# Gate matrix of a PEER layer: third block kept in SBUF, the others stored in 4 KB runs and fetched by four tiles, with new places for loads and dots

## What is computed

```python
def _peer(x, w_query, sub_keys, w_down, w_up):       # x: 512 tokens x 1024
    q = (x @ w_query).reshape(n_tok, 8, 2, 128)
    sc = einsum('thpk,hpnk->thpn', q, sub_keys)        # 8 heads, 2 sides, 128 keys
    va, ia = top_k(sc[:, :, 0], 16); vb, ib = top_k(sc[:, :, 1], 16)
    cand = va[..., :, None] + vb[..., None, :]
    top, flat = top_k(cand, 16)
    expert = ia[flat // 16] * 128 + ib[flat % 16]      # 128 experts per token, of 16384
    gate = softmax(top)
    act = gelu(einsum('tkd,td->tk', w_down[expert], x))
    return einsum('tk,tkd->td', gate * act, w_up[expert])
x = layernorm(alpha * x + peer(x))
```

## Time and profile before

| | |
|---|---|
| median of 3 executions | 1749.91 us (1749.54 to 1751.03) |
| profiled execution, time / span | 1752.79 / 1751.0 us |
| busy, share of span: TensorE, VectorE, ScalarE, GpSimd | 92%, 70%, 36%, 46% |
| moved by DMA | 428 MB, mean 244 GB/s |
| mean granted TensorE clock | 0.963 of full |
| down stage in `peer_block` / up stage (matmuls) | 526 to 1188 / 1206 to 1731 us |

### The profile page before, as it was taken

How to read it: one execution, slowest core, us unless ns; L and a number is a source line. 1 busy time by engine, 2 the same in 40 slices (tenths; PEclk the granted TensorE clock), 3 DMA queues, 4 the chain that set the end, 5 groups by cost and what they waited for, 6 DMA issues and landing times.

```text
span 1751.0 us, 22553 instructions
## 1 busy us (share of the span) xinstructions
PE 1610.9 (92%) x8252; PEld 1435.8 (82%) x8252; DVE 1233.3 (70%) x2110; ACT 623.1 (36%) x807; POOL 799.1 (46%) x468
## 2 busy tenths in 40 slices
PE   7999978869979999998999899685999999999995
PEld 6787857758869999998999899674888888888884
DVE  2643442256989889788978895346888888888887
ACT  4223324222224355443544454132333333333331
POOL 7443642123318866686568566675222222222220
PEclk9999989889999999999999999897999999999997
DMA  8422322114226776797679667999999999999993
GB/s 296 156 96 85 117 76 96 34 50 146 83 66 188 260 245 200 245 364 263 205 257 362 248 201 272 372 347 386 376 352 355 357 355 351 355 354 354 355 351 147
DMA packets 195414, 428.08 MB, mean 244 GB/s; under 512 B 17009, under 2 KB 116593, under 8 KB 194801
## 3 DMA queue, kind: packets, MB, share of 16 engines
q1 hardware_dynamic: 106944, 262.78, 43.2%
q0 software_dynamic: 36864, 134.23, 21.0%
q10 hardware_dynamic: 51504, 29.71, 5.6%
HBM read 372.13 MB, written 54.53 MB: 244 GB/s over the span
## 4 chain that ended last, share of the span: by engine, by line
PE 53%; DMA 3%; ACTq 2%; POOL 2%; issue 1%; DVE 1%; ACT 0%; DVEq 0%
PE ps L1178 10%; PE ps L1179 10%; PE ps L1180 10%; PE ps L892 6%; PE ps L894 6%; PE ps L893 6%; PE ps L1150 3%; PE ps L1152 2%; ACTq L1086 2%; DMA gate_d<-gmat 2%; DMA rows<-in_w_down,expert 1%; POOL w_lo L1029 1%; POOL rows L1037 1%; DVE gmat L1353 0%; DVE gmat L1350 0%
## 5 line engine op out<-in xcount | busy, mean ns | idle before, releaser
L1029 POOL TENSOR_TENSOR w_lo<-raw,w_hi 128x1024 fp32r<-128x1024 f32 x127 | 324.9, 2564 | 186.4 <-ACT w_hi L1061 185.8
L892 PE MATMUL ps<-b_hi,w_hi 128*128 128x384 f32 x1024 | 354.4, 346 | 33.6 <-POOL w_lo L1029 33.6
L1061 ACT ACTIVATE w_hi<-raw 128x1024 fp32r<-128x1024 f32 x252 | 266.5, 1057 | 319.8 <-PE ps L1180 315.9
L893 PE MATMUL ps<-b_lo,w_hi 128*128 128x384 f32 x1024 | 347.7, 340 | 0.0
L894 PE MATMUL ps<-b_hi,w_lo 128*128 128x384 f32 x1024 | 347.6, 339 | 0.0
L1178 PE MATMUL ps<-w_hi,b_hi 128*128 128x512 f32 x768 | 299.9, 390 | 18.5 <-DVE b_lo L1268 18.5
L1037 POOL DMA_INDIRECT rows<-in_w_up,expert x128 | 128.9, 1007 | 386.8 <-DVE ps L1275 378.9
L1179 PE MATMUL ps<-w_lo,b_hi 128*128 128x512 f32 x768 | 299.5, 390 | 0.0
L1180 PE MATMUL ps<-w_hi,b_lo 128*128 128x512 f32 x768 | 299.5, 390 | 0.0
L182 POOL TENSOR_TENSOR w_lo<-raw,w_hi 128x1024 fp32r<-128x1024 f32 x60 | 152.9, 2556 | 199.2 <-ACT w_hi L210 199.2
L1197 DVE SCALAR_TENSOR_TENSOR rows<-rows,ps 128x1024 f32<-128x1024 f32 x128 | 155.0, 1219 | 107.5 <-DMA rows<-in_w_down,expert 100.9
(11 more groups left out here) (205 smaller groups left out, 2572.1 us busy)
## 6 DMA issues: line engine op xcount, KB each, us to landing
raw<-in_down_t SPq DMA_DIRECT2D x128, 512.0 KB, 3.8
raw<-in_up_t SPq DMA_DIRECT2D x128, 512.0 KB, 5.4
raw<-in_units SPq DMA_DIRECT2D x76, 512.0 KB, 3.2
act_d<-act_t SPq DMA_DIRECT2D x128, 192.0 KB, 4.4
gate_d<-gmat ACTq DMA_DIRECT2D x48, 512.0 KB, 10.1
gmat<-act_d SPq DMA_DIRECT2D x128, 192.0 KB, 4.6
gmat<-gate_d SPq DMA_DIRECT2D x128, 192.0 KB, 5.8
xt_raw<-in_x_t SPq DMA_DIRECT2D x1, 2048.0 KB, 12.3
```

Source lines behind the costliest of these rows:

```text
L892: nc.tensor.matmul(out, ring.w_hi[:, s, w], b_hi[:, c, 0:DT], start=c == 0, stop=False)
L893: nc.tensor.matmul(out, ring.w_hi[:, s, w], b_lo[:, c, 0:DT], start=False, stop=False)
L1029: nc.gpsimd.tensor_tensor(w_lo[:, s, :], raw[:, s, :], w_hi[:, s, :].bitcast(F32), ALU.subtract).then_inc(split_done, 1)
L1061: nc.scalar.activation(w_hi[:, u % W4, :], raw[:, u % W4, :], ACT.Copy).then_inc(hi_done, 1)
```

## The change

In words. (1) Only blocks 0 and 1 (`KEPT = 2`) of the gate matrix are stored, as runs of 4 KB in each partition, two pieces a tile in the first eight tiles of the following block; block 2 stays in `gmat`. (2) The stored gates are fetched for four tiles by one 512 KB DMA into the arrays `v16` and `i16` by turns, the activations by a DMA a tile into five slots `h_t` in `c0`. (3) The product is made in place, in two instructions, one for blocks 0 and 1, one for block 2. (4) The first loads of the up stage are issued at down tile 104 and not 123. Activations and gates then have new places in SP's loop. (5) Each block has 14 dots before its gate rounds instead of 8; `low(0)` and `low(1)` stand before the last seven dots. (6) The start value of `acc` comes from `xb` in PSUM and not from a load of `x_d`; the copy of `xb` stands behind tile 3 and not ahead of tile 0. (7) `xres` and the norm's weights use the part of `gmat` whose tiles are done, and are loaded at up tile 112.

```diff
-        steps += [t0 + 4, t0 + 6, t0 + 8, t0 + 10] + [t0 + 12, t0 + 13, t0 + 14, t0 + 15]
+        steps += [t0 + i for i in (4, 4, 5, 5, 7, 7, 8, 8, 13, 13, 14, 14, 15, 15)]
...
-            def load_gated(j):
-                if j >= W4:
-                    sp.wait_ge(h_ready, j - W4 + 1)
+            def load_act(j):
+                if j >= HS:
+                    sp.wait_ge(h_split, j - HS + 1)
                 sp.wait_ge(act_stored[j % ACTS], 16 * (j // ACTS) + 16)
-                sp.dma_start(act_u[:, j % W4, :], t["act_d"][j]).then_inc(ag_full[j % W4], 16)
-                sp.dma_start(gate_u[:, j % W4, :], t["gate_d"][j]).then_inc(ag_full[j % W4], 16)
+                sp.dma_start(h_t[:, j % HS, :], t["act_d"][j]).then_inc(act_full[j % HS], 16)
+
+            def load_gates(g):
+                if g >= 2:
+                    sp.wait_ge(h_ready, 2 * GG * (g - 1))
+                sp.dma_start(gate_u[g % 2], t["gate_d"][:, :, g * GG * P:(g + 1) * GG * P].rearrange(
+                    "b a (u j) -> a b u j", u=GG)).then_inc(gate_full[g % 2], 16)
...
-                if u == TILES - 5:
-                    sp.wait_ge(gate_stored, 16 * PIECES * DB)
-                    for j in range(W4):
-                        load_gated(j)
-                    sp.dma_start(xres[:, GB, :], t["x2_d"][GB]).then_inc(xg_full, 16)
-            for j in range(W4, 2 * W4):
-                load_gated(j)
-            for j in range(TILES - 2 * W4):
-                load(TILES + j + 2 * W4)
-                load_gated(j + 2 * W4)
+                if u == TILES - 24:
+                    sp.wait_ge(picks_ready, DB)
+                    sp.wait_ge(gate_stored, 16 * PIECES * KEPT)
+                    load_gates(0)
+                    load_gates(1)
+                    for j in range(HS):
+                        load_act(j)
+            for j in range(TILES):
+                if j + 2 * W4 < TILES:
+                    load(TILES + j + 2 * W4)
+                if j + HS < TILES:
+                    load_act(j + HS)
+                if j % GG == GG - 1 and j // GG + 2 < TILES // GG:
+                    load_gates(j // GG + 2)
+                if j == TILES - 16:
+                    sp.wait_ge(h_ready, 2 * late_tiles)
...
-                if u >= LEAD + BLOCK_TILES and b < DB and i < PIECES:
-                    store_piece(b - 1, i)
-                if b == DB and i < PIECES // 2:
-                    store_piece(DB - 1, 2 * i)
-                    store_piece(DB - 1, 2 * i + 1)
-                if u == TILES - 2:
+                if u >= LEAD + BLOCK_TILES and b < DB and i < PIECES // 2:
+                    store_piece(b - 1, 2 * i)
+                    store_piece(b - 1, 2 * i + 1)
+                if u == TILES - 8:
                     h_high(0)
                     h_high(1)
...
-                top_experts(nc, step, done, k, b, lambda: dots_until(made[0] + 1))
+                top_experts(nc, step, done, k, b, lambda: dots_until(made[0] + 2))
...
-                dots_until(first + 8)
+                dots_until(first + 14)
...
             def product(j):
...
+                of = h_t[:, s, :].rearrange("p (b j) -> p b j", b=DB)
+                nc.vector.scalar_tensor_tensor(out=of[:, 0:KEPT, :], in0=of[:, 0:KEPT, :], scalar=1.0 / GSCALE,
+                                               in1=gate_u[g % 2][:, :, j % GG, :], op0=ALU.mult, op1=ALU.mult
+                                               ).then_inc(h_ready, 1)
+                nc.vector.scalar_tensor_tensor(out=of[:, KEPT, :], in0=of[:, KEPT, :], scalar=1.0 / GSCALE,
+                                               in1=gmat[:, j, :], op0=ALU.mult, op1=ALU.mult).then_inc(h_ready, 1)
```

More of the change, by code:

```diff
@@ L882 @@
 PIECES = 16
+HS = 5
+GG = 4
+KEPT = DB - 1
 PB = NK // PIECES
@@ L951, in peer_block @@
         acc = ps[:, XB:XB + 2, :]
+        h_t = c0[:].rearrange("p h c -> p (h c)")[:, 0:HS * DT].rearrange("p (s j) -> p s j", s=HS)
+        gate_u = [x[:].rearrange("p b s i -> p (b s i)").rearrange("p (b u j) -> p b u j", b=KEPT, u=GG)
+                  for x in (t["v16"], t["i16"])]
         flat_g = gmat[:].rearrange("p b j -> p (b j)")
[L954 to L957, removed]
+        xres = flat_g[:, 0:TB * D].rearrange("p (b d) -> p b d", b=TB)
+        lng, lnb = flat_g[:, TB * D:TB * D + D], flat_g[:, TB * D + D:TB * D + 2 * D]
+        late_tiles = (TB + 2) * D // P
         def h_slot(of, s):
@@ L973, in peer_block @@
         gate_stored = sem("gate_stored")
-        ag_full = [sem(f"ag_full{i}") for i in range(W4)]
+        act_full = [sem(f"act_full{i}") for i in range(HS)]
+        gate_full = [sem(f"gate_full{i}") for i in range(2)]
         h_ready, h_hi_done, h_split = sem("h_ready"), sem("h_hi_done"), sem("h_split")
-        coef_done, xg_full, x2_full, ln_full = sem("coef_done"), sem("xg_full"), sem("x2_full"), sem("ln3_full")
+        coef_done, x2_full, ln_full = sem("coef_done"), sem("x2_full"), sem("ln3_full")
+        xb_full = sem("xb_full")
         block_done, res_added = sem("block4_done"), sem("res4_added")
@@ L1085, in store_piece @@
                     act.wait_ge(half_free, halves * (b + 1))
[L1086 to L1087 removed]
+                act.dma_start(t["gate_d"][b, :, PB * i * P:(PB * i + PB) * P],
+                              gmat[:, PB * i:PB * i + PB, :].rearrange("p b j -> p (b j)")).then_inc(gate_stored, 16)
             def h_high(j):
[L1090 removed]
+                act.wait_ge(h_ready, 2 * j + 2)
                 if j >= 2:
                     act.wait_ge(tile_done, TILES + max(0, j - W4 + 1))
[L1093 removed]
+                nc.scalar.activation(h_slot(b_hi, j % W4), h_t[:, j % HS, :].rearrange("p (b j) -> p b j", b=DB),
                                      ACT.Copy).then_inc(h_hi_done, 1)
[L1096 to L1097 removed]
             for u in range(TILES):
@@ L1101, in _ @@
                 b, i = divmod(u - LEAD, BLOCK_TILES)
+                if u == W4 - 1:
+                    act.wait_ge(xb_full, 16)
+                    nc.scalar.activation(xb.rearrange("p i (c j) -> p (i c) j", j=P), xb_in, ACT.Copy
+                                         ).then_inc(xb_ready, 1)
                 if u == LEAD - 2:
@@ L1205, in _ @@
             made = [0]
-            dve.wait_ge(const_full, 32)
+            dve.wait_ge(const_full, 16)
             step(nc.vector.tensor_copy(numbers[:], k["iota"][:].unsqueeze(2).broadcast_to([P, P, RJ])))
@@ L1256, in _, with split_low @@
                 dots_until(made[0] + 4)
-            dots_until(HK - 4)
             def product(j):
[L1260 to L1263, removed]
+                s, g = j % HS, j // GG
+                dve.wait_ge(act_full[s], 16 * (j // HS) + 16)
+                dve.wait_ge(gate_full[g % 2], 16 * (g // 2) + 16)
+                of = h_t[:, s, :].rearrange("p (b j) -> p b j", b=DB)
[4 more added lines that the diff above has]
+                                               in1=gmat[:, j, :], op0=ALU.mult, op1=ALU.mult).then_inc(h_ready, 1)
             def low(j):
-                s = j % W4
                 dve.wait_ge(h_hi_done, j + 1)
-                nc.vector.tensor_tensor(h_slot(b_lo, s), h_t[:, s, :].rearrange("p (b j) -> p b j", b=DB),
-                                        h_slot(b_hi, s).bitcast(F32), ALU.subtract).then_inc(h_split, 1)
+                nc.vector.tensor_tensor(h_slot(b_lo, j % W4), h_t[:, j % HS, :].rearrange("p (b j) -> p b j", b=DB),
+                                        h_slot(b_hi, j % W4).bitcast(F32), ALU.subtract).then_inc(h_split, 1)
+            def split_low(u):
+                s = u % W4
+                dve.wait_ge(hi_done, u + 1)
+                nc.vector.tensor_tensor(w_lo[:, s, :], raw[:, s, :], w_hi[:, s, :].bitcast(F32),
+                                        ALU.subtract).then_inc(split_done, 1)
             def row(j):
@@ L1283, in split_low @@
                                         ALU.subtract).then_inc(split_done, 1)
+            dots_until(HK - 16)
+            dve.wait_ge(half_free, halves * DB)
             for j in range(3):
                 product(j)
-            dots_until(HK)
+            dots_until(HK - 7)
             low(0)
             low(1)
-            dve.wait_ge(xg_full, 16)
+            dots_until(HK)
             dve.wait_ge(row_free, HK)
-            step(nc.vector.tensor_scalar(acc, xres[:, GB, :].rearrange("p (i c) -> p i c", i=2), ALPHA, None, ALU.mult))
+            step(nc.vector.tensor_scalar(acc, xb, ALPHA, None, ALU.mult))
             dve.wait_ge(coef_done, 1)
```

10 lines of the change are left out of this document (5 added, 5 removed).

## The result

| | before | after |
|---|---|---|
| median | 1749.72 us (4 executions) | 2081.28 us (2076.93 to 2086.43) |
| ratio after / before | | 1.189, 95% interval 1.187 to 1.191 |
| span of the profiled execution | 1751.0 us | 2075.2 us |
| first up matmul | 1206.4 us | 1172.5 us |
| first to last up matmul | 524 us | 882 us |

The kernel is 19% slower, in the way that the prediction described and by more than its range allowed: 1966 was forecast, with 2075 as the upper end. The down stage gave back 34 us and not 70, and the up stage took 358 us more and not 286.

What follows compares the result with a forecast made beforehand. TensorE was taken to bound the up stage at 4.08 us a tile. Down stage 70 us shorter, but 120 up tiles at 6.49 us behind late activation loads, plus ends: about 1966 us, range 1925 to 2075.

Steps and rivals of the forecast that it cites:

- full-load landing: Rival, up stage: loads land as slowly as at full load, 8.0 us a tile, 2146 us; chance 6%.
- PE at its slow clock throughout: Rival, up stage: idle time drops PE to 1.2 GHz, 7.68 us a tile, about 2138 us; chance 5%.
- a load in time after all: Rival, up stage: activation load issued a whole iteration earlier than counted, PE stays the bound at 4.08, 1680 us; chance 3%.
- half of the loop hidden: Rival, up stage: something unseen hides half of the loop, between 1700 and 1925 us; chance 5%.
- The gate term: Up stage: every fourth tile's 512 KB gate load, queued behind the activation load, adds 1.9 us, 0.48 a tile.
- The base of 6.01 us: Up stage: one loop iteration without gate load, 0.02 to issue, 3.7 landing, 2.29 for waking up and VectorE work.
- The loads for the norm: Late up stage: 2.5 MB for the final norm queued ahead of one activation load, adding 5 us.
- 6+17+30+29-12 = 70: Down stage: start, stores, third block kept, moved dots, less dot costs; up stage starts 70 us earlier, bounds 55 and 82.
- The dots: Down stage: two more dots before each block's first gate round cost 7 to 15 us over three blocks, taken as 10.
- The stores: Down stage: 4 KB runs done by tile 8 end ScalarE's two waits of 19.5 us; gain 17 us.
- The last 20 tiles: End of down stage: no late stores gains 30 us, fewer dots left gains 29, GpSimd's remaining gathers cost 2.
- The start: Start of down stage: wait for `x_d` leaves ScalarE's path, 5.3 of 11.3 us idle stay; gain 6 us.

Runs made afterwards that it cites:

- both loads in time: Changed kernel with up-stage activation and gate loads issued with the four-iteration lead of the kernel before: 1712.46 us, ratio 0.978 to the kernel before.
- late loads: Kernel before, only its up-stage activation and gate loads behind raw load 128+j+8 made those of tile j+5 instead of j+8: 2120.83 us.
- run without gathers: Changed kernel with the gathers of w_up rows in the up stage left out, so the fourth block's sum differs: 2026.24 us.
- old dots: Kernel with activation and gate loads at their old lead, but 8 dots a block as before the change, 44 left for the last 20 tiles: 1716.10 us.
- The best version here: Kernel with activation and gate loads at their old lead, but 12 dots a block, four where VectorE waits for ScalarE's exponent: 1699.49 us, ratio 0.971.

## Why the prediction was right, and where it was wrong

**The mechanism was right.** `product(j+5)` needs a load that SP issues behind the split before it. There are 120 such iterations, the undisturbed one takes 6.02 us (forecast 6.01), the kernel is slower, and undoing this alone makes it faster than the one before (both loads in time), while doing it alone ruins the old kernel (late loads). The rivals fell: no full-load landing (3.4 us median, not 4.6), no PE at its slow clock throughout (granted 0.88, busy 71%, VectorE waited for DMA and PE for VectorE). The Trainium skill's rule (DMA: Bandwidth & Descriptors, Rules for kernel authors: issue early, wait late) is what this change broke, and the runs bear it out. The estimate worked out from the Trainium skill's fit (DMA: Bandwidth & Descriptors, Anatomy of one DMA), 6.26 us a tile with gates, is below the measured 7.11, as mine of 6.49 was. The two other rivals, a load in time after all and half of the loop hidden, gave 1680 us and at most 1925.

**The range was missed by 6 us, the point by 115: three terms of the sum were mis-sized.** The low end of the range adds up to 1923 and not 1925, which changes nothing. In the profiled executions (span 2075.2 against 1966.8, 108 us):

1. *The gate term, "I take 1.9, or 0.48 a tile".* A gate tile takes 9.34 us on the mean and not 7.9: 30 x 1.43 = 43 us. I had let the gate load land 1.9 us behind the act load, but it is issued 0.43 us later and lands a median of 5.6 us after its issue. The run without gathers shows 1.1 us of each gate tile to be the gathers' share, the rest its own.
2. *The base of 6.01 us, from a median landing.* Undisturbed tiles do take that, but the mean of all others is 6.28: 0.27 x 89 = 24 us. The loads for the norm cost 7 and not 5. A closed loop pays for every late landing, and nothing in it evens them out. This is the same error as in the expectation for the old kernel with late loads.
3. *"6+17+30+29-12 = 70" for the down stage.* 33.9 was measured, and the first up matmul came at 1172.5. "A down stage that ends after 1160 (the moved dots cost more)" stood among the signs of being wrong, and it came. By the table above:
   - *The dots cost 27 us and not 10.* This is the largest error of the down stage. The run with both loads in time needs 527.9 us for the three blocks, the one with the old dots 500.6. I had counted the dots behind the picks and overlooked the eight inside the search, where four had been. Their gathers took 9.9 us (median, 755 to 800) to land, against 7.5 (735 to 800) before, VectorE waited for them in the middle of the search (8.0 us in four waits, in the second block), and the picks came late: PE waits 14.0 us for them and 8.9 for the first gate rounds.
   - *The stores gave 7.5 us and not 17.* With the old dots the blocks need 500.6 us, before they needed 508.1.
   - *The last 20 tiles gave 50 us and not 57.* Nothing is left to gain there: PE is busy 80.00 of 80 and 11.86 of 12.5 us. I had charged the slow clock to whole stretches, their idle time included. On PE's busy time alone, 13% of 60.65 and 17% of 25.21 us, it would have been 12 us and not 18.
   - *The start gave 3.8 us and not 6.* PE's idle time there fell from 11.58 to 5.49 us, as forecast, but the tiles ahead of it ended 2.6 us later (517.30 against 514.68), in a part that the change leaves alone. That is the scatter seen in the first column, and no effect.

Terms 1 and 2 make 72 us with those 2 us for the norm and some 3 of rounding in the ends of the stage, term 3 makes 36.

That the second product instruction costs nothing was right (0.65 us of spare time left). So was the undisturbed tile, down to its parts: from the raw load's issue to the product 3.76 us, forecast 3.7 and 0.05; no run shows the 0.05 for waking up by itself.

## What to carry to other kernels

When a load moves in a queue that runs in order, write down for each load the event that releases its issue and the event that needs it, in iterations of the engine that makes both: under one iteration of distance the loop closes on itself, with four slots (late loads) as with five (the change). Price such a loop by the mean landing under its own traffic, with each queued load's own issue and landing, not by medians. And moving work from one crowded place to another is a trade to be summed at both ends. The best version here puts four dots where VectorE had waited for ScalarE (16.3 us with the old dots); six there made the picks late again.

## What was not expected of the hardware

At 197 GB/s of traffic and a DMA share of 0.60 the landing of a 192 KB load still varies from 3.2 to 5.6 us, and the loop with 192 KB gate loads in the kernel before, fastest 6.4 us, has iterations up to 10. Taking the gathers away removed the late landings of the gate loads and the latest of the act loads (4.4 us at most), but left the mean of the other tiles at 6.18 us. What makes the remaining late ones was not found.
